# mLSTM gate rows held as high and low parts in eight rows, and spread over the partitions by one fp32r pass each

## The reference, cut to what matters

```python
ig = igb + b_if[l, :H_B]          # 4 heads
fg = fgb + b_if[l, H_B:]
lfc = jax.nn.log_sigmoid(gates(fg))
b = jnp.cumsum(lj, axis=-1)
logD = b[..., :, None] - b[..., None, :] + ij[..., None, :]
m_row = jnp.maximum(inter, jnp.max(logD, axis=-1))
Dm = jnp.exp(logD - m_row[..., None])
Sm = jnp.einsum('bhjd,bhsd->bhjs', qj, kj) * Dm
h = num / jnp.maximum(jnp.abs(den), jnp.exp(-m_row))[..., None]
```

## Time and profile before

| | us |
|---|---|
| median of 3 runs (2457.89 to 2461.23) | 2457.97 |
| the profiled execution | 2455.18 |
| its span | 2453.1 |
| PE busy | 2318.1 |
| DVE busy | 1157.5 |
| POOL busy | 987.8 |
| ACT busy | 705.6 |

### The profile page before, as it was taken

How to read it: one execution, slowest core, us unless ns; L and a number is a source line. 1 busy time by engine, 2 the same in 40 slices (tenths; PEclk the granted TensorE clock), 3 DMA queues, 4 the chain that set the end, 5 groups by cost and what they waited for, 6 DMA issues and landing times.

```text
span 2453.1 us, 27542 instructions
## 1 busy us (share of the span) xinstructions
PE 2318.1 (94%) x9990; PEld 1762.4 (72%) x9990; DVE 1157.5 (47%) x1201; ACT 705.6 (29%) x1097; POOL 987.8 (40%) x789
## 2 busy tenths in 40 slices
PE   7999999899899999999999879999999998999998
PEld 5777755477788888888877656666676675888776
DVE  5774455545733433334337875465455444411223
ACT  4243355522311111111123423333423433200121
POOL 3533400186544444444436632222254451444340
PEclk9999999999999999999999999999999999999999
DMA  5111100222111111111112300000011110111121
GB/s 196 44 40 38 35 1 9 86 86 78 61 43 51 51 43 51 47 47 51 43 52 71 129 26 26 26 26 26 26 35 38 39 43 18 52 43 51 53 102 69
DMA packets 31186, 125.84 MB, mean 51 GB/s; under 512 B 3464, under 2 KB 3848, under 8 KB 30224
## 3 DMA queue, kind: packets, MB, share of 16 engines
q1 hardware_dynamic: 28656, 103.26, 13.0%
q10 hardware_dynamic: 2464, 21.66, 2.2%
HBM read 112.33 MB, written 12.58 MB: 51 GB/s over the span
## 4 chain that ended last, share of the span: by engine, by line
PE 81%; DVE 9%; ACT 4%; issue 4%; DMA 1%; POOL 1%; SPq 0%; DVEq 0%; ACTq 0%; POOLq 0%
PE PG L607 14%; PE PG L613 13%; PE PG L612 13%; PE PG L1134 5%; PE PG L1140 5%; PE PG L1139 4%; PE PG L954 2%; PE PG L1180 2%; PE PO L981 1%; PE PO L1203 1%; PE PT L968 1%; PE PO L1277 1%; PE PG L660 1%; PE PG L666 1%; PE PG L665 1%
## 5 line engine op out<-in xcount | busy, mean ns | idle before, releaser
L522 POOL TENSOR_TENSOR WH<-WR,zero 128x512 fp32r<-128x512 f32 x376 | 417.0, 1109 | 1335.1 <-PE PG L607 705.6
L525 POOL TENSOR_TENSOR WL<-WR,WH 128x512 fp32r<-128x512 f32 x376 | 535.2, 1423 | 29.4
L607 PE MATMUL PG<-HH,WH 128*128 128x512 f32 x1232 | 486.9, 395 | 3.7 <-issue 1.4
L613 PE MATMUL PG<-HH,WL 128*128 128x512 f32 x1232 | 480.4, 390 | 0.0
L612 PE MATMUL PG<-HL,WH 128*128 128x512 f32 x1232 | 480.1, 390 | 0.0
L607 PEld LDWEIGHTS PG<-HH,WH 128*128 128x128 f32 x1232 | 231.7, 188 | 58.5 <-issue 6.1
L612 PEld LDWEIGHTS PG<-HL,WH 128*128 128x128 f32 x1232 | 231.7, 188 | 49.7 <-issue 2.2
L613 PEld LDWEIGHTS PG<-HH,WL 128*128 128x128 f32 x1232 | 231.7, 188 | 48.7
L1134 PE MATMUL PG<-HH,WH 128*128 128x512 f32 x544 | 230.2, 423 | 5.4 <-ACTq L1881 2.8
L1140 PE MATMUL PG<-HH,WL 128*128 128x512 f32 x544 | 213.5, 392 | 0.0
L1139 PE MATMUL PG<-HL,WH 128*128 128x512 f32 x544 | 212.6, 391 | 0.0
(11 more groups left out here) (458 smaller groups left out, 3938.0 us busy)
## 6 DMA issues: line engine op xcount, KB each, us to landing
WR<-weights SPq DMA_DIRECT2D x188, 512.0 KB, 3.4
X<-x_spill ACTq DMA_DIRECT2D x2, 4096.0 KB, 12.4
RAW<-x SPq DMA_DIRECT2D x8, 512.0 KB, 7.8
x_spill<-X ACTq DMA_DIRECT2D x1, 4096.0 KB, 12.8
x_spill<-X ACTq DMA_DIRECT2D x4, 1024.0 KB, 5.0
y<-RAW ACTq DMA_DIRECT2D x8, 512.0 KB, 2.8
POSI<-positions ACTq DMA_DIRECT2D x1, 512.0 KB, 15.1
sqf<-squares SPq DMA_DIRECT2D x1, 256.0 KB, 2.6
```

The costliest lines, as they stand in the source:

```text
L522: pool.tensor_tensor(WH[:, slot, part], WR[:, slot, part], zero[:, :].to_broadcast([P, HALF]), ALU.add).then_inc(w_hi, 1)
L525: pool.tensor_tensor(WL[:, slot, part], WR[:, slot, part], WH[:, slot, part].bitcast(F32), ALU.subtract).then_inc(w_split, 1)
L607: m = pe.matmul(out[:, cut], WH[:, slot, w], hi[:, cut], start=n == 0, stop=False)
L613: m = pe.matmul(out[:, cut], WL[:, slot, w], hi[:, cut], start=False, stop=last)
```

## The change

GR and selM become fp32r. Each row of GR is now held twice: rows 0 to 3 of a group hold the value rounded to fp32r (the high part), rows 4 to 7 what is missing from it (the low part). To have both, the gate rows are computed twice, in eight partitions, by the same instructions (the weights, the biases and all of GROWS have eight rows). selM has two ones, for the high and the low row, so that one fp32r matmul adds the two parts.

```diff
-        GR = at("GR", 156, [P, S])
-        GROWS = [RAW[0:4, n, :] for n in (0, 1, 2, 3, 6, 7)]
+        GR = at("GR", 156, [P, S], F32R)
+        GROWS = [RAW[0:8, n, :] for n in (0, 1, 2, 3, 6, 7)]
+        GHIGH = RAW[0:8, 1, :].bitcast(F32R)
-        selM = at("selM", 25, [P, 2, P])
+        selM = at("selM", 25, [P, 2, P], F32R)
...
-            turn_halves(hb, 4, GR)
+            turn_halves(hb, 4, GR[:, :].bitcast(F32))
...
-            act.activation(GROWS[5], g.psum(0)[0:4, :], ACT.Identity, bias=vec[0:4, gb:gb + 1])
+            act.activation(GROWS[5], g.psum(0)[0:8, :], ACT.Identity, bias=vec[0:8, gb:gb + 1])
...
+            def high_and_low(rows, high, out):
+
+                step(dve.tensor_copy(high, rows))
+                return dve.scalar_tensor_tensor(out, high.bitcast(F32), v("low_rows")[0:8], rows,
+                                                ALU.mult, ALU.add)
...
+            def gate_inputs():
+
+                step(high_and_low(GROWS[5], GHIGH, GR[64:72, :]))
+
             def gate_maxima():
 
-                step(dve.tensor_copy(GR[64:68, :], GROWS[5]))
-                step(dve.tensor_scalar(GR[0:4, :], GROWS[4], -1.0, None, ALU.mult))
-                step(dve.tensor_tensor(GROWS[3], GROWS[3], GROWS[4], ALU.add))
-                dve.tensor_scalar(GR[32:36, :], GROWS[3], -1.0, None, ALU.mult).then_inc(gate_rows, 1)
+                step(dve.scalar_tensor_tensor(GROWS[3], GROWS[3], -1.0, GROWS[4], ALU.mult, ALU.subtract))
+                step(dve.tensor_scalar(GROWS[4], GROWS[4], -1.0, None, ALU.mult))
+                step(high_and_low(GROWS[4], GHIGH, GR[0:8, :]))
+                high_and_low(GROWS[3], GHIGH, GR[32:40, :]).then_inc(gate_rows, 1)
...
-                    ins = dve.tensor_copy(selM[:, n, :], col.to_broadcast([P, P]))
+                    ins = dve.tensor_tensor(selM[:, n, :], high.to_broadcast([P, P]),
+                                            low.to_broadcast([P, P]), ALU.add)
...
             DiffHead(0).tile(1)
+            gate_inputs()
+            DiffHead(0).tile(2)
             gate_maxima()
-            DiffHead(0).tile(2)
...
-                dve.tensor_copy(ACOL[:, 4 * (m % 2):4 * (m % 2) + 4, :],
-                                hb.bank(m).rearrange("p (t n) -> p t n", t=4)[:, :, 64:68])\
-                   .then_inc(hb.free(m), 1)
+                part = ACOL[:, 4 * (m % 2):4 * (m % 2) + 4, :]
+                turned = hb.bank(m).rearrange("p (t n) -> p t n", t=4)
+                step(dve.tensor_copy(part, turned[:, :, 64:68]))
+                dve.tensor_tensor(part, turned[:, :, 68:72], part, ALU.add).then_inc(hb.free(m), 1)
```

More of the change, by code:

```diff
@@ L90 @@
            ("norm_a", 4), ("norm_b", 4), ("inv_freq", 1), ("phase", 1), ("turn", 1), ("sign", 1),
-           ("eps", 1)]
+           ("eps", 1), ("low_rows", 1)]
 VEC0, NVEC = starts(VECTORS)
@@ L1761, in _ @@
             gb = VEC0["gate_bias"]
-            act.activation(GROWS[5], g.psum(0)[0:4, :], ACT.Identity, bias=vec[0:4, gb:gb + 1])
-            act.activation(GROWS[0], g.psum(0)[32:36, :], ACT.Identity,
-                           bias=vec[32:36, gb:gb + 1]).then_inc(g.free(0), 1)
+            act.activation(GROWS[5], g.psum(0)[0:8, :], ACT.Identity, bias=vec[0:8, gb:gb + 1])
+            act.activation(GROWS[0], g.psum(0)[32:40, :], ACT.Identity,
+                           bias=vec[32:40, gb:gb + 1]).then_inc(g.free(0), 1)
             g.ready(act, 1)
@@ L2639, in _ @@
             chain_low(3, KT - 1)
-            step(dve.memset(GR[:, :], 0.0))
+            step(dve.memset(GR[:, :].bitcast(F32), 0.0))
             dve.wait_ge(lam_loaded, 16)
@@ L2701, in select @@
                     c = 32 * n
-                    col = (ident[:, c:c + 1] if isinstance(head, int) else ident[:, bass.ds(head + c, 1)])
-                    ins = dve.tensor_copy(selM[:, n, :], col.to_broadcast([P, P]))
+                    high, low = ((ident[:, x:x + 1] if isinstance(head, int) else ident[:, bass.ds(head + x, 1)])
+                                 for x in (c, c + 4))
+                    ins = dve.tensor_tensor(selM[:, n, :], high.to_broadcast([P, P]),
+                                            low.to_broadcast([P, P]), ALU.add)
                     if n == 0:
@@ L3040, in _weights @@
     g8 = w2[:, 4608:4616].reshape(KT, P, 8).transpose(1, 0, 2)
-    gates[0, :, :, 0:4] = g8[:, :, 0:4]
-    gates[0, :, :, 32:36] = g8[:, :, 4:8]
+    for at in (0, 4):
+        gates[0, :, :, at:at + 4] = g8[:, :, 0:4]
+        gates[0, :, :, 32 + at:36 + at] = g8[:, :, 4:8]
     heads = _blocks(w2, [tile(part * 512 + n * P) for n in range(4) for part in range(4)])
@@ L3088, in _vectors @@
             put("ffn_conv", 8 * t + 4 * part + 3, a["ffn_conv_b"][0, at:at + P])
-    put("gate_bias", 0, a["b_if_2"][0, 0:4])
-    put("gate_bias", 0, a["b_if_2"][0, 4:8], 32)
+    for at in (0, 4):
+        put("gate_bias", 0, a["b_if_2"][0, 0:4], at)
+        put("gate_bias", 0, a["b_if_2"][0, 4:8], 32 + at)
     for n in range(ML_HEADS):
@@ L3105, in _vectors @@
     put("eps", 0, np.full(P, EPS, np.float32))
+    put("low_rows", 0, -np.ones(4, np.float32), 4)
     return out
```

## The result

The changed kernel takes 2464.86 us (median of 17 runs, 2459.89 to 2468.82); the kernel before took 2456.69 in the same series (17 runs, 2449.79 to 2461.23). The ratio is 1.0034, with a 95% interval of 1.0027 to 1.0042: the change makes the kernel slower by 8.2 us at the medians. The forecast 2461.9 was 3.0 too low, and the difference of 3.9 us that it foresaw is half of the one measured.

What follows compares the result with a forecast made beforehand. PE was taken to bound nearly everywhere, ACT's queue at the spreads and DVE in the first attention head. Wait +2.8, clock +2.3 and spreads -1.2 gave +3.9 us on 2457.97, so 2461.9 us; range 2456.8 to 2466.0.

Steps and rivals of the forecast that it cites:

- likeliest case: Whole kernel: the forecast itself, +3.9 us to 2461.9 us, chance 0.5.
- the upper end: Range's top: rival (3), slow casts and long clock dip, with one dip more, cut at 2466.0 us.
- What the change does: At the spreads: one record of about 0.39 us for each, 16 in all.
- the rival with two records: At the spreads: each stays at two records, +2.8 + 2.3, 2463.1 us; chance 0.03.
- the one in which PE's work comes back whole: At the spreads: 12 x 0.64 = 7.7 us of PE's work come back, 2450.3 us; chance 0.05.
- The wait in the first attention head: Before tile 2's transposes: PE waits for DVE's six gate instructions and resumes 2.8 us later.
- the term from the row (1.7): First attention head: POOL's pair running beside DVE's gate instructions adds 1.7 us to them.
- The clock behind that wait: First attention head: after about 5 us idle PE's clock falls to 1.2 GHz, costing +2.3 us.
- What PE gains at the spreads: Before mLSTM heads 1 to 3: the fill starts 0.41 us earlier a head, -1.2 us; head 0 nothing.
- rival (5): mLSTM: a shift in time removes or adds a clock dip, widening every case by 1.7 us; no chance given.
- Rival (3): Both costs at upper bounds: casts at the slow price and long clock dip, +6.2 us, 2464.2; chance 0.2.
- Rival (1): First attention head: POOL's pair falls beside the wait, the clock doesn't fall; -0.1 us, 2457.9; chance 0.22.

Runs made afterwards that it cites:

- fp32: The changed kernel with the 16 spreads run as fp32 again, all of DVE's new work kept; 2456.54 us, ratio 1.0009 to the kernel before.
- two: The changed kernel with each fp32r spread issued twice; 2458.33 us, ratio 1.0010 to the kernel before.
- three: The changed kernel with each fp32r spread issued three times into the same half bank; 2456.41 us, ratio 1.0005 to the kernel before.
- last five: The changed kernel with three of a group's four spreads issued once and the last five times; 2456.33 us, ratio 1.0004 to the kernel before.
- four rows: The kernel before with GR and selM as fp32r, low parts left out and DVE's order as before; 2459.67 us, ratio 1.0016.
- three changed ones with the gates later: The changed kernel with gate operations after tiles 4, 5 and 6 of the first attention head; spreads once 2458.69 us, three times 2452.63, twice 2454.11.
- before with gates later: The kernel before with only its four gate operations moved behind tile 4 of the first attention head; 2453.31 us, ratio 0.9984.
- changed kernel with gates later: The changed kernel with head 0's eight gate operations moved behind tiles 4, 5 and 6 of the first attention head; 2458.69 us, ratio 1.0012.

## Why the prediction was right or wrong

The time fell inside the range, but above the likeliest case's own span (2459.5 to 2464), and the verdict is slower, for which it gave 0.35. That it fell inside is luck: the upper end was made for slow casts and one dip more, and what filled it was a cost of 5.7 us that the sum didn't have. Step by step:

**What the change does** was right: 16 records for 32, of 0.50 us where about 0.39 was foreseen; the rival with two records falls, and so does the one in which PE's work comes back whole. DVE's operations on eight rows last what they did on four (CAST 0.67, with one tensor 0.68, with two 1.21 to 1.28 alone). `select` costs 0.62 for 0.49, 0.13 longer (0.14 foreseen).

**The wait in the first attention head** was right, nearly to its parts. From the end of tile 2's normalisation to the maximum of tile 3 passed 7.55 us (1440.95 to 1448.50), 7.56 foreseen; PE waits 5.07 us (5.1) and resumes 26.39 us after the first scores for 23.70: +2.7 for +2.8. POOL's pair added 0.74 to the CAST and 0.90 to the other (1.42 and 2.17 less 0.68 and 1.27), 1.64 us for 1.7; POOL's own two took 3.55 us for 2.33. So both engines paid, and the term from the row (1.7) was the better one than the full 2.33. By the Trainium skill (SBUF — State Buffer, "Who interferes with whom") the instruction that starts first holds the shared ports for its whole length and the other stands still. The trace agrees: DVE's instruction at 1443.55 had begun before POOL's WH and kept its 1.27 us, and WH was the one stretched. Then WH, the CAST, WL and DVE's last instruction took turns: each ended 0.13 to 0.19 us earlier than its own length alone (1.04, 0.68, 1.29, 1.27) behind the end of the one before. What was too high was my working from the page, which put all of POOL's pair on DVE, though DVE held the ports first and WH served part of its time in that wait.

**The clock behind that wait** fell as foreseen. Window behind it in the changed kernel:

```profile
1446.16:1451.23 5.07, 0.00 (x1) 0.01 (x1) 4.90 (x8) 1.45 (x4) 1.23 (x1) 0.97 0.00 0
1451.23:1454.60 3.37, 3.37 (x10) 2.22 (x11) 0.67 (x2) 0.49 (x1) 0.00 (x0) 0.53 0.02 5
```

Half clock lasted some 3.4 us, not 4.8 or 6.1. Head 0 grew by 4.14 us, of which 2.69 is the wait; the rest, 1.45, is what the dip cost, for 2.3 foreseen. Both terms together: 4.1 measured, 5.1 predicted.

**What PE gains at the spreads** is the step that failed, in size and then in sign. The size: I let MN begin at 1838.17, 0.02 us behind ACT's read of V. ACT takes 0.17 us from one instruction to the next there, where its program waits for its own result; the same 0.17 stood in the earlier trace rows at the table load. With it MN begins 0.15 later and a head gains 0.26, as measured (4.77 to 4.52), not 0.41: -0.8 us over three heads for -1.2. The sign: I wrote that behind the spreads "the fills are PE's own time, so it isn't given back", and asked only what PE's time is worth there, not what PE's work is worth. Taking 1.8 us of work out of a stretch that ACT paces leaves PE busy 2.00 us of 4.52 for 3.83 of 4.77, and the half clock that comes with it cost 13.67 - 11.06, 12.56 - 11.06 and 12.63 - 11.01 us, together 5.7. A row pointed to it: behind 1.8 us of idle in the mLSTM stage the clock averaged 0.64, which rival (5) took as chance that a shift in time may add or remove once. It came in all nine groups with one pass, and in none of 24 others. With -0.8 + 5.7 for -1.2 the prediction's sum is 2.7 + 1.45 - 0.8 + 5.7 = +9.1; the medians say +8.2.

**The rest.** The two stages of the profiles give +9.8, more than the medians' +8.2, since the profiled execution of before (2455.18) lies 1.5 below its median and that of after (2465.62) 0.8 above: 4.1 in head 0 and 1.2 in the other attention heads (a dip, below), 4.9 at the groups, less 0.5 elsewhere in the mLSTM stage. Rival (3), 2464.2, has the right time for the wrong reasons: neither the CASTs nor the dip behind the wait were at their upper bounds. Rival (1) falls with the wait of 5.07 us.

**What stays open.** The kernels with the changed place of the gates and no dips at the spreads (fp32, two, three, last five) have an attention stage 5.3 to 7.2 us longer than before, an mLSTM stage 1.3 to 2.9 us shorter, yet medians only 0.6 us below to 1.7 above. The two stages give +3.3 to +4.4 for each profiled execution. The mLSTM stage of the kernel before has in its profile a dip more (1945 to 1949) than theirs has. For the kernel with fp32 spreads the clock of all executions says the same: its mean is 0.9839 (12) for 0.9829 before (35). By estimate 0.0010 of the span is 4.9 us at half clock, worth some 2.5 us, so a part of its longer attention stage comes back as less half clock elsewhere. For the three others the means differ from those of the kernel before by 0.0004 or less, in one case downwards, and settle nothing. So the price of the attention part alone in the median, between -2 and 5 us by these intervals (0.9993 to 1.0021), isn't settled; nor is why the single pass costs more beside it (8.3 us from the kernel with fp32 spreads to the changed one) than without it (3.4, four rows against before).

## What to carry to other kernels

Before you shorten an engine's work in a stretch that another engine paces, ask what that work was keeping up: PE's work there cost no time, and here the clock of the fill behind it hung on it. The cheap test is to issue the short matmul two or three times; if the kernel gets faster, put other useful work of PE in the gap, or leave the longer form. And look where preparatory operations stand in the queue of the engine that bounds a short stage: moving four of them by three tiles shortened that head by 2.0 us and gave a ratio of 0.9984 (0.9973 to 0.9995), while the change made the kernel slower.

## What the runs showed of the hardware

Several waits of 0.3 to 1.6 us can bring the half clock where no long one is: at the spreads of head 1 PE's idle stretches are 0.35, 0.32, 0.28 and 1.56 us, and the clock falls; with 0.36, 0.31, 0.28 and 0.65, and five passes before the last, it stays. The Trainium skill tells, of another kernel in bf16, that short idle stretches between groups of matmuls made the clock go down and up (TensorE: Matmul & The Clock Gate, "A second HAM failure mode: psum-queue depth-cycling"), and the trace agrees: the clock fell at nine of nine groups with one pass.

One and the same wait can end either way. In the second attention head PE waits 1.94 us for DVE in both kernels; windows of 4 us behind it, of before, then of after:

```profile
1523.50:1527.50 4.00, 4.00 (x16) 2.55 (x17) 3.68 (x5) 0.60 (x3) 1.19 (x2) 1.00 0.00 0
```

```profile
1528.50:1532.50 4.00, 4.00 (x10) 1.95 (x11) 2.81 (x3) 0.42 (x2) 0.00 (x0) 0.62 0.00 0
```

PE gets 16 matmuls done in one and 10 in the other. Each of the five kernels with the gates in the changed place shows this dip, and so do the three changed ones with the gates later (there the wait is 1.85 us); before, four rows, and before with gates later don't. In the third attention head the same wait of 1.94 us stands in all eleven kernels, and a dip follows it in two: spreads twice, and before with gates later. So the time from the first scores alone doesn't decide it: before with gates later and the changed kernel with gates later take nearly the same 81.06 and 81.08 us to the end of head 0, and the first has its dip in the third head, the other in the second. What decides is open. The head with such a dip is 0.9 to 1.7 us longer than in the kernel before, which no sum over instructions shows beforehand.

A CAST from fp32 to fp32r of 8x1024 on DVE takes 0.67 us, about as the copy of 4x1024 in fp32 did (0.69), and 1.42 to 1.66 beside a working POOL.
